# State-space layers of a hybrid decoder: the weight block cut into pieces with the mixer between them

## The reference, cut to what matters

```python
z, xbc, dt = jnp.split(h @ w_in, [D_INNER, D_INNER + CONV_DIM], axis=-1)
conv = conv_b + sum(ext[:, k:k + L] * conv_w[k] for k in range(CONV_W))
xs, bs, cs = jnp.split(jax.nn.silu(conv), ...)
cb = jnp.einsum('bcign,bcjgn->bcgij', c, b)                  # per group, within a chunk of tokens
w = cb[:, :, :, None] * jnp.exp(segsum(adt))                 # adt = softplus(dt + bias) * a
y_diag = jnp.einsum('bcgrij,bcjgrp->bcigrp', w, xdt)
states = jnp.einsum('bcjgn,bcgrj,bcjgrp->bcgrpn', b, decay_states, xdt)
new_states = decayed old states + states
y_off = jnp.einsum('bcign,bcgrpn,bcgri->bcigrp', c, new_states[:, :-1], jnp.exp(a_cum))
y = rmsnorm((y + xh * d_skip) * silu(z), per group of 512) @ w_out
```

## Time and profile before

| | us |
|---|---|
| median of 3 runs | 2619.59 (2611.56 to 2623.01) |
| the profiled execution | 2618.41 |
| its span, first to last instruction | 2616.6 |
| TensorE busy | 2363.0, 90% |
| VectorE / ScalarE / GpSimd busy | 1225.5 / 992.4 / 450.4 |
| mean granted clock of TensorE | 0.884 |

### The profile page before, as it was taken

How to read it: one execution, slowest core, us unless ns; L and a number is a source line. 1 busy time by engine, 2 the same in 40 slices (tenths; PEclk the granted TensorE clock), 3 DMA queues, 4 the chain that set the end, 5 groups by cost and what they waited for, 6 DMA issues and landing times. The chain is left out here.

```text
span 2616.6 us, 38501 instructions
## 1 busy us (share of the span) xinstructions
PE 2363.0 (90%) x15187; PEld 2047.0 (78%) x15187; DVE 1225.5 (47%) x2074; ACT 992.4 (38%) x1497; POOL 450.4 (17%) x396
## 2 busy tenths in 40 slices
PE   6999997999896698999876799699988999979999
PEld 5877776999794455999874466599988877859999
DVE  5644444555433233654346433355546544445554
ACT  2534444443333111543344211444335434354442
POOL 2112120243100000442100000033310112202430
PEclk9888786999996698999995699899998878779999
DMA  5343332666750342656630445166674334225554
GB/s 159 97 118 99 101 85 73 170 167 176 258 160 23 78 113 67 177 162 200 218 113 19 170 160 194 33 174 168 182 250 133 108 100 125 75 66 159 164 152 140
DMA packets 505013, 352.44 MB, mean 135 GB/s; under 512 B 13517, under 2 KB 486367, under 8 KB 504133
## 3 DMA queue, kind: packets, MB, share of 16 engines
q1 hardware_dynamic: 503822, 323.01, 42.4%
q10 hardware_dynamic: 1024, 27.13, 2.7%
HBM read 326.59 MB, written 50.63 MB: 144 GB/s over the span
## 5 line engine op out<-in xcount | busy, mean ns | idle before, releaser
L243 PE MATMUL ps<-xh,wh 128*128 128x288 f32 x2368 | 676.4, 311 | 41.8 <-issue 24.9
L221 DVE TENSOR_TENSOR wl<-raw,wh 128x2048 fp32r<-128x2048 f32 (+3 forms) x241 | 503.9, 2092 | 354.7 <-ACT wh L213 350.2
L243 PE MATMUL ps<-xl,wh 128*128 128x288 f32 x2368 | 667.2, 306 | 0.0
L213 ACT ACTIVATE wh<-raw 128x2048 fp32r<-128x2048 f32 (+3 forms) x241 | 419.7, 1744 | 293.1 <-PE ps L248 183.4
L243 PEld LDWEIGHTS ps<-xh,wh 128*128 128x128 f32 x2368 | 474.9, 201 | 45.2 <-issue 41.1
L243 PEld LDWEIGHTS ps<-xl,wh 128*128 128x128 f32 x2368 | 473.8, 200 | 0.4
L248 PE MATMUL ps<-xh,wl 128*128 128x288 f32 x2368 | 340.1, 297 | 0.0
L248 PEld LDWEIGHTS ps<-xh,wl 128*128 128x128 f32 x2368 | 324.2, 189 | 0.0
L457 POOL TENSOR_TENSOR gh<-sg,ut 128x288 f32<-128x288 f32 x88 | 216.7, 2463 | 351.3 <-ACT sg L395 351.3
L243 PE MATMUL ps<-hh,wh 128*128 128x288 f32 x704 | 194.4, 301 | 17.2 <-issue 15.4
L243 PE MATMUL ps<-hl,wh 128*128 128x288 f32 x704 | 192.9, 300 | 0.0
(11 more groups left out here) (312 smaller groups left out, 3214.7 us busy)
## 6 DMA issues: line engine op xcount, KB each, us to landing
raw<-in_ffn_w_in SPq DMA_DIRECT2D x176, 512.0 KB, 5.1
raw<-in_ssm_w_in SPq DMA_DIRECT2D x80, 512.0 KB, 4.8
raw<-in_ffn_w_out SPq DMA_DIRECT2D x64, 384.0 KB, 4.8
raw<-in_ffn_w_out SPq DMA_DIRECT2D x64, 320.0 KB, 3.4
H<-in_state_ssm SPq DMA_DIRECT2D x32, 512.0 KB, 4.3
out_ssm_sample<-H SPq DMA_DIRECT2D x32, 512.0 KB, 3.2
raw<-in_ssm_w_out SPq DMA_DIRECT2D x32, 512.0 KB, 5.2
Kp<-in_cache_diff_k SPq DMA_DIRECT2D x64, 256.0 KB, 4.1
```

The costliest lines, as they stand in the source:

```text
L213: act.activation(wts["hi"][:, s, 0:width], raw[:, s, 0:width], ACT.Copy).then_inc(hi_ready.sem, 1)
L221: dve.tensor_tensor(wts["lo"][:, s, 0:width], raw[:, s, 0:width], wts["hi"][:, s, 0:width].bitcast(F32), ALU.subtract).then_inc(lo_ready.s ...
L243: pe.matmul(out, W[0][:, kk, j, :], x_[:, k, :], stop=False, start=(part == 0 and kk == 0 and x_ is seg.hi), skip_group_check=True)
```

## The change

`block_mm` becomes a generator of sixteen pieces (`block_pieces`), eight of 4 matmuls and eight of 2. In the state-space phase TensorE now draws one or two pieces between the steps of the mixer, and the front of chunk k and the rest of chunk k-1 lie in slot k beside block k. The order of the blocks becomes dt, first x pair, four of B and C, then x and z in turn; the last is a z pair, and slot 15 has no block. The blocks use banks 0 to 3 in turn, both heads' spreads, the chunk's spread and the sums of squares bank 6, turned states and chunk sums bank 5, turned x and outer product bank 4. The outer product takes `US` (high, low and again high part of the scaled x of the samples, in 96 rows) and `Bm` made from `BtS` (high, high, low part of B), both in the single-pass type. `split_u` and `split_b` make them. `y_state`, `y_inside` and `decay` are cut in halves. The sums of squares wait at slots 6, 10 and 14, and what waits for the root is the spread of slots 7, 11 and 15. The tail's transposes use banks 0 to 3, two of six before the last chunk.

```diff
-    def block_mm(pe, seg, i):
+    def block_pieces(pe, seg, i):
...
+            yield
         pe.wait_ge(lo_ready.sem, g + 1)
...
+            if end:
+                mm.then_inc(blocks_done.sem, 1)
+            yield
...
+                for m in range(4, 9):
+                    seg, i = block_of(m)
+                    load_block(sp, seg.lin, i, b0 + m)
+                for k in range(CI + 2):
+                    m = k + 9
+                    if b0 + m <= last:
+                        seg, i = block_of(m)
+                        load_block(sp, seg.lin, i, b0 + m)
...
+                    if k >= 2:
+                        store_state(k - 2)
...
                 def turn_x(c):
...
+                        pe.wait_ge(updated.sem, updated.at(NB * (c - 1)))
...
                 def spread(h):
+                    c = h // 2
+                    pe.wait_ge(e_ready.sem, e_ready.at(3 * h))
...
+                    if h % 2 == 0 and c >= 7:
+                        pe.wait_ge(y_logged.sem, y_logged.at((c - 3) // 4))
...
+                    out = ps[:, 6, 0:TOK]
...
                 def sums_of_chunk(c):
...
+                    pe.wait_ge(h_moved.sem, h_moved.at(2 * c + 2))
...
                 def outer_half(c, half):
                     pe.wait_ge(bm_ready.sem, bm_ready.at(c // 4 + 1))
+                    pe.wait_ge(us_lo.sem, us_lo.at(c + 1))
+                    pe.wait_ge(us_hi.sem, us_hi.at(2 * c + 2))
+                    pe.wait_ge(xu_ready.sem, xu_ready.at(min(3 * (c + 2), 3 * CI)))
                     pe.wait_ge(updated.sem, updated.at(NB * c + 4 * half))
-                    pe.matmul(ps[:, 3, :], XU[0:NS, c % 2, 6, :], Bm[:, 4 * half:4 * half + 4, :],
+                    pe.matmul(ps[:, 4, :], US[:, c % 2, :], Bm[:, 4 * half:4 * half + 4, :],
...
+                for k in range(1, CI):
+                    L = block_pieces(pe, *block_of(2 + EARLY + k)) if k < CI - 1 else iter(())
+                    more(L)
+                    sums_of_chunk(k - 1)
+                    more(L)
+                    turn_x(k)
+                    more(L)
+                    y_state(k - 1, 0)
+                    more(L)
+                    y_state(k - 1, 1)
+                    more(L)
+                    spread(2 * k)
+                    spread_chunk(k)
+                    more(L)
+                    outer_half(k - 1, 0)
+                    more(L)
+                    turn_state(k, 0)
+                    more(L)
+                    y_inside(k - 1, 0)
+                    more(L, 2)
+                    spread(2 * k + 1)
+                    more(L, 2)
+                    y_inside(k - 1, 1)
+                    more(L, 2)
+                    outer_half(k - 1, 1)
+                    more(L)
+                    turn_state(k, 1)
+                    more(L)
+                    y_across(k - 1)
+                    if k % 4 == 2 and k >= 6:
+                        g = k // 4 - 1
+                        pe.wait_ge(e_ready.sem, e_ready.at(6 * k + 6))
+                        sum_squares(g, range(4 * g, 4 * g + 4))
...
+                def split_u(c):
+                    act.wait_ge(xu_ready.sem, xu_ready.at(3 * (c + 1)))
...
+                    for q in (0, 2):
+                        act.activation(US[q * NS:(q + 1) * NS, c % 2, :], XU[0:NS, c % 2, 6, :], ACT.Copy).then_inc(
+                            us_hi.sem, us_hi.inc())
...
+                for k in range(CI):
+                    what, n = drained_in(k)
+                    ahead(g0 + k + 1)
...
+                        move_s0(k - 1)
+                        move_fs(k - 1)
+                    if what == "x":
+                        taps(n)
+                    else:
+                        silu_z(n)
+                    split_u(k)
...
+                    if k % 4 == 3 and k >= 7:
+                        root(k // 4 - 1)
+                    if k + 1 < CI:
+                        pick_rows(k + 1)
+                    decay_chunk(k)
+                    decay(2 * k)
+                    move_state(k, 0)
+                    decay(2 * k + 1)
...
+                    if what == "x":
+                        silu(n)
+                    if k % 2 and k >= 3:
+                        square(k - 3)
+                        square(k - 2)
+                    move_state(k, 1)
...
+                def split_u(c):
+                    dve.wait_ge(us_hi.sem, us_hi.at(2 * c + 1))
...
+                    dve.tensor_tensor(US[NS:2 * NS, c % 2, :], XU[0:NS, c % 2, 6, :], US[0:NS, c % 2, :].bitcast(F32),
+                                      ALU.subtract).then_inc(us_lo.sem, us_lo.inc())
...
+                for k in range(CI):
+                    what, n = drained_in(k)
+                    if k >= 2:
+                        take(k - 2)
+                    if what == "x":
+                        scale_xb(n)
+                    else:
+                        scale_z(n)
+                    spread_x(k)
+                    ahead(g0 + k + 1)
+                    split_u(k)
...
+                    if k % 2 and k >= 3:
+                        gate(k - 3)
+                        gate(k - 2)
+                    if k >= 1:
+                        update(k - 1, 0)
+                    if what == "x":
+                        more_taps(n)
...
+                    if k >= 1:
+                        update(k - 1, 1)
```

More of the change, by code:

```diff
@@ L836, in ssd @@
                         lambda o: (z_scaled, z_scaled.at(o // 2 + 1)),
-                        places=[b0 + 2 + EARLY + 2 * i for i in range(PAIRS)], banks=lambda i, j: j)
-            g0 = b0 + 1 + EARLY
-            last = b0 + EARLY + 2 * PAIRS
+                        places=[g0 + 2 * i + 1 for i in range(PAIRS - 1)] + [g0 + CI - 2],
+                        banks=lambda i, j: (0 if i == PAIRS - 1 else 2) + j)
+            last = g0 + CI - 2
             stream["block"] = last + 1
@@ L1033, in y_state @@
                     pe.wait_ge(y_taken.sem, y_taken.at(c))
-                    for b in range(NB):
+                    if c == 0:
+                        pe.wait_ge(cb_ready.sem, cb_ready.at(2 * GROUPS))
+                    for b in range(4 * half, 4 * half + 4):
                         at = TOK + P + b * T
@@ L1054, in y_across @@
                               start=True, stop=True, skip_group_check=True).then_inc(yoff_mm.sem, yoff_mm.inc())
-                def sum_squares(g, k):
-                    pe.wait_ge(squared.sem, squared.at(4 * g + 4))
-                    drained(k)
-                    for c in range(4):
-                        mm = pe.matmul(ps[:, 1, 0:TOK], ones, sq[:, c, :], start=(c == 0), stop=(c == 3))
-                    mm.then_inc(sq_summed.sem, sq_summed.inc())
-                    bank_free[1] = (y_logged, y_logged.at(g + 1))
@@ new lines, in turn_tail @@
+                def turn_tail(q):
+                    pe.wait_ge(tail_ready.sem, tail_ready.at(CX))
+                    if q in (2, 3):
+                        pe.wait_ge(z_scaled.sem, z_scaled.at(PAIRS))
+                    if q >= 4:
+                        pe.wait_ge(tl_moved.sem, tl_moved.at(q - 3))
+                    for k in range(4):
+                        mm = pe.transpose(ps[0:27, (q + 2) % 4, k * P:(k + 1) * P], tail[:, 4 * q + k, :, :], ident)
+                    mm.then_inc(tl_mm.sem, tl_mm.inc())
@@ new lines, in more @@
+                def more(L, n=1):
+                    for _ in range(n):
+                        next(L, None)
+                L = block_pieces(pe, *block_of(2 + EARLY))
+                more(L)
+                turn_x(0)
+                more(L)
+                turn_b(0)
+                more(L)
+                turn_b(1)
+                more(L)
+                spread(0)
+                spread_chunk(0)
+                more(L)
+                turn_b(2)
+                more(L)
+                turn_b(3)
@@ new lines, in _ @@
+                sums_of_chunk(CI - 1)
+                y_state(CI - 1, 0)
+                y_state(CI - 1, 1)
+                outer_half(CI - 1, 0)
+                y_inside(CI - 1, 0)
+                outer_half(CI - 1, 1)
+                y_inside(CI - 1, 1)
+                y_across(CI - 1)
+                pe.wait_ge(e_ready.sem, e_ready.at(3 * HEADS))
+                pe.wait_ge(ea_ready.sem, ea_ready.at(CI))
+                sum_squares(GROUPS - 1, (CI - 4, CI - 3))
+                for q in range(2, 6):
+                    turn_tail(q)
@@ L1316, in _ @@
+                move_tail(0)
+                move_tail(1)
+                move_s0(CI - 1)
+                move_fs(CI - 1)
+                for q in range(2, 6):
+                    move_tail(q)
+                square(CI - 2)
+                square(CI - 1)
                 root(GROUPS - 1)
```

458 lines of the change are left out of this document (226 added, 232 removed).

## The result

The changed kernel takes 2480.8 us (median of 4, 2474.3 to 2491.8), the one before on the same chip 2621.3 us (median of 4); the ratio is 0.947, 95% interval 0.942 to 0.952. The forecast was 2484. The profiled execution has a span of 2483.4 us for 2616.6.

What follows compares the result with a forecast made beforehand. TensorE was taken to set the pace in the state-space slots, with time lost to half clock. Per layer, slots -55, start -6 and end -6 us make 67, 134 for both: 2618.4 - 134 = 2484 us, range 2435 to 2570.

Steps and rivals of the forecast that it cites:

- The outer product: Two products per chunk, stacked halves at 0.35 us each for 1.05: 19.6 us saved in a layer's fourteen slots.
- the 22.7 named as the most: Upper end of the outer product's saving in a layer's fourteen slots, range 0 to 22.7 us.
- The interleaving: Mixer steps between block pieces: waits of 0.6 us per slot on average, 8.4 us a layer (0 to 30).
- The path followed to the end of the odd slot: VectorE's taps end 12.2 us in, then silu, squares and state move to 15.9; chunk sums about 1 us late.
- The case named for no wait at all: Lower end of the interleaving's cost: 0 us if silu's table load runs before its wait.
- The place named as tight: Odd slot's end, where the next chunk sums wait for ScalarE's second state move, about 1 us late.
- The clock: Fourteen slots of a layer: 10 us lost to half clock in place of 43 (0 to 80).
- The rule on groups that cycle through PSUM banks: Small pauses between bank groups swing TensorE's clock; would bring about the slow-clock rival, 2664 us, chance 0.06.
- Roots: Two waits of 6.2 us before blocks go; ScalarE is late next, 1 us at each of three roots.
- Start and end: State-space phase outside the fourteen slots, per layer: start -6 us (-12 to +6), end -6 us (-10 to 0).
- the rival: ScalarE and VectorE become the bound in the slots, 17.5 us a slot: 2536 us, chance 0.20.
- The clean case: Nothing late and the clock holds: fourteen slots 207 us, 91 us saved per layer, 2436 us, chance 0.14.

Runs made afterwards that it cites:

- two experiments, one from each side: Changed kernel with the outer product back in float32: 2551.2 us, ratio 0.977; kernel before with only the outer product changed: 2516.5 us, ratio 0.958.
- the reordered kernel: Changed kernel with y_state's second half moved behind the first outer product and four moves in ScalarE's queue: 2457.6 us, ratio 0.936; run again 2452.0 us.
- the repetition: The changed kernel run once more on the same chip, nothing altered: 2478.1 us, ratio 0.945.
- the kernel with the added copy: Changed kernel with every second state move on ScalarE done twice: 2487.0 us, ratio 0.949.

## Why the prediction was right, step by step

**The outer product.** Right in direction, mis-sized: 0.23 us for 0.35, and 0.46 us per slot in the neighbours that the sum did not have. At full clock it takes 1.8 us off a slot (two experiments, one from each side; 1.6 in some slots of one of them), about 25 in fourteen, and not 19.6. That is above the 22.7 named as the most: the bound was taken from the product's own rows, and the price of a step is also in what it does to the steps around it. The Trainium skill ("FP8 and Floating Point Precision", "TensorE Precision Notes") has true FP32 as four passes. The trace comes near it: 1.05 us against 0.23 is 4.6 times.

**The interleaving.** Its price was put into waits, 0.6 us a slot. The waits were a quarter of that: 0.5 at each of the two roots, 0.2 at each odd-to-even joint. The path followed to the end of the odd slot was wrong. It had VectorE's taps as the last to come, 12.2 us in, with silu behind them. They are done 10.8 us in, and what silu waits for is ScalarE's own work before it, the second head's exponentials and the spread that these need from TensorE. The state move then ends 14.7 us in, where the forecast had 15.9. The case named for no wait at all, the table load ahead of silu's wait, doesn't occur either, since the input is there before the load starts. The place named as tight was the right one all the same: doubling the move there shows at once.

In place of the waits stand the joints, which the sum had at nothing. From the outer product alone (13.94) to the reordered kernel (14.50) the block's rows go from 6.47 to 7.65 us and the mixer's from 7.5 to 6.85: +0.6 a slot. In the fourteen slots the errors are 6 us too little saving for the product, 6 us too much for waits (2.3 by the rows, for 8.4), and some 8 us of joints left out. That they cancel within 4, so that 225 meets 224.1, is luck.

**The clock.** 10 us of loss in fourteen slots was forecast; the slots with a spell over those like them without sum to 10.6 in layer 0 and 6.0 in layer 3 (5.9 and 9.1 in the repetition). The mechanism is borne out in the main. TensorE is busy throughout at seven of the ten falls; two come 1.5 us behind the wait of 0.5 at a root, and slot 1 of layer 0 carries on what began behind the wait in slot 0. The low clock is back in 27 of 28 slots with the blocks whole, and with the two halves of y_state further apart it is gone from all but the root slots and one slot 1. Between these ends the count of slots with a spell goes the same way: 15 with the halves side by side, 10 and 9 with one piece between, 5 further apart, 2 when the waits are mended too. Single counts prove little, though: the kernel with the added copy has TensorE's order of the changed one, and 5. What the forecast did not see is that a shorter outer product by itself also costs less clock (0.89 for 0.83), so the two parts of the change share one gain and don't add up: alone they bring 107 us (outer product) and 66 us (all the rest), together 141 to 145 and not 173. The rule on groups that cycle through PSUM banks (the Trainium skill, "TensorE: Matmul & The Clock Gate", "A second HAM failure mode") was weighed and given 0.06. No run here supports it: the kernel with thirteen returns from a mixer bank to a block bank in each slot is granted 0.99, that with one 0.80.

**Roots.** The two waits of 6.2 us are gone, as forecast. Late next is ScalarE, as forecast, with 0.5 for 1 us in slots 7 and 11, but with 3.0 for 1 at the third root, in slot 15, outside the fourteen. With half of y_state moved behind the spread the first two wait 1.9 us, 1.4 more: the time of that half and its block piece had covered the root.

**Start and end.** -4.5 and -5.2 us for -6 each. The wait before the token sums, 3.68 us, was to stay about as long; it is 0.95 in layer 0 and 1.9 in layer 3. The start has a new wait of 3.89 us on ScalarE in slot 0, the one that was expected there without a number. 13.7 us of half clock follow it in layer 0 of the first profile, 3.4 in its layer 3 and in both layers of the repetition. The end keeps its wait for the last root and norm (11.8 us), and no experiment was made on it.

**The rivals.** None of the slots is bound by ScalarE or VectorE, but the rival had 0.20 with reason: the added copy shows a margin of 0.2 us at most at the joints. The clean case is added up wrong: 280 - 207 with 12 and 10 for start and end is 95 us a layer and not 91, which gives 2428 and not 2436. The best order, with no wait in its slots, stands at 2452 to 2458. Its layer 0 has 64.4, 210.4 and 40.2 us for start, slots and end, where that sum has 60.7, 207 and 36.9. So a third of what is missing lies in the slots, in the joints and a spell of half clock in slot 1, and two thirds in start and end.

## What to carry to other kernels

Where a trace shows the clock fall with the engine busy, look for thin steps side by side and put dense ones between; count the time at half clock per slot, with and without, before an engine's waits. When steps are cut into pieces, price each return to the dense stream from a row (0.09 us here, 0.62 for 0.53), and price a step with its neighbours. After a gain on the bounding engine, look first at the queue of the engine that now releases it. Here y_state further apart brought nothing measurable alone (2476.8 for 2480.8 and 2478.1), and with it the moves in ScalarE's order, all of work that was there already, brought 20 us. The whole interleaving brought 38 on top of the outer product. The moves without y_state's were not run.

## What the runs showed that was not expected

- In the changed kernel the spells of half clock fall in different slots in layer 0 and layer 3 of one execution, and in others again in its repetition, though the instructions are the same. With the outer product alone they fall in the same slots in both layers. The times of one kernel spread by 10 to 34 us, and part of this lies in the attention layers, which no kernel here touches.
- A float32 product between block pieces, 0.8 us longer each time, doesn't cost clock: 0.96 against 0.94 to 0.97. The theory that longer thin stretches bring more falls had expected a loss.
- GpSimd's product of 128x288 takes 0.80 us in the changed kernel and took 1.50 before. With the outer product alone, in the old order, it takes 0.87. This hides behind TensorE in all of them, and the cause was not looked for. The groups by line and form, fourteen slots, before and after:

```profile
L1134 POOL TENSOR_TENSOR E<-E,cb 128x288 f32<-128x288 f32 x30 | 44.4, 1500 | 153.7 <-ACT E L1260 153.7
```
```profile
L1235 POOL TENSOR_TENSOR E<-E,cb 128x288 f32<-128x288 f32 x30 | 23.9, 797 | 189.7 <-ACT E L1374 169.1 <-ACT cb L1325 20.6
```
